# An expert's tokens by an indirect row transfer and transposes in place of a gather by products

## The reference

```python
def moe_swiglu(u, w_router, b_router, w_gate, w_up, w_down):
    tok = u.reshape(bn * s, d)
    logits = tok.astype(f32) @ w_router.astype(f32) + b_router.astype(f32)
    top_val, top_idx = lax.top_k(logits, TOP_K_EXPERTS)
    gates = jax.nn.softmax(top_val, axis=-1)
    combine = jnp.einsum('tk,tke->te', gates, jax.nn.one_hot(top_idx, N_EXPERTS, dtype=f32))
    out = jnp.zeros((bn * s, d), f32)
    for e in range(N_EXPERTS):
        out = out + combine[:, e:e + 1] * swiglu(tok, w_gate[e], w_up[e], w_down[e]).astype(f32)
    return out.astype(u.dtype).reshape(bn, s, d)
```

## Time and profile before

| what | value |
| --- | --- |
| median of 3 runs | 1637.91 us (1637.24 to 1638.79) |
| the profiled execution | 1632.35 us, span 1630.5 us |
| PE, PE weight loads | busy 94%, 73% of the span |
| DVE, ACT, POOL | busy 77%, 64%, 4% |
| DMA | 469.68 MB, mean 288 GB/s |
| PE's share of the chain that ended last | 81% |

### The profile page before, as it was taken

The page is one execution under the profiler, slowest core; times in us unless marked ns, Lnnn a source line. Parts: engine busy times, 40 slices in busy tenths (PEclk is TensorE's granted clock), DMA queues, the critical chain, the costliest instruction groups (busy, mean ns, idle before and its releaser), DMA issues.

```text
span 1630.5 us, 22147 instructions
## 1 busy us (share of the span) xinstructions
PE 1538.7 (94%) x7571; PEld 1195.2 (73%) x7572; DVE 1254.6 (77%) x1707; ACT 1048.2 (64%) x1381; POOL 62.8 (4%) x90
## 2 busy tenths in 40 slices
PE   4999989999799969999999999999999999999997
PEld 2645468887675458888888888888888888888885
DVE  6896345543682249899899889889989989989987
ACT  3105444443548437787788788788788778778775
POOL 5351000000000000000000000000000000000000
PEclk9999999999899969999999999999999999999998
DMA  9625876544458458999999999999989999999960
GB/s 321 239 104 199 317 283 212 178 179 166 150 178 309 156 219 308 348 353 359 337 356 351 367 340 343 367 334 348 379 321 352 364 332 367 348 337 362 357 255 27
DMA packets 203752, 469.68 MB, mean 288 GB/s; under 512 B 5108, under 2 KB 11558, under 8 KB 203574
## 3 DMA queue, kind: packets, MB, share of 16 engines
q1 hardware_dynamic: 202656, 466.80, 78.8%
q0 software_dynamic: 400, 1.09, 0.3%
q10 hardware_dynamic: 646, 1.16, 0.2%
HBM read 467.98 MB, written 1.05 MB: 288 GB/s over the span
## 4 chain that ended last, share of the span: by engine, by line
PE 81%; ACT 5%; DVE 4%; issue 2%; ACTq 0%; DVEq 0%
PE ps L810 23%; PE ps L812 22%; PE ps L811 22%; PE ps L816 2%; PE ps L1370 2%; DVE w_lo L1949 2%; PE ps L1329 2%; PE ps L1083 1%; ACT work L1845 1%; PE ps L835 1%; ACT uT L1601 1%; ACT w_hi L1588 1%; ACT uT L1610 1%; PE ps L1439 0%; PE ps L1440 0%
## 5 line engine op out<-in xcount | busy, mean ns | idle before, releaser
L1949 DVE TENSOR_TENSOR w_lo<-ring,w_hi 128x1024 fp32r<-128x1024 f32 (+2 forms) x572 | 668.0, 1200 | 118.1 <-ACT w_hi L1588 99.0
L1588 ACT ACTIVATE w_hi<-ring 128x1024 fp32r<-128x1024 f32 (+2 forms) x572 | 595.4, 1045 | 215.2 <-PE ps L812 211.8
L810 PE MATMUL ps<-w_hi,e_hi 128*128 128x512 f32 x896 | 356.6, 398 | 9.7 <-DVE w_lo L1949 9.7
L812 PE MATMUL ps<-w_hi,e_lo 128*128 128x512 f32 x896 | 350.5, 391 | 0.0
L811 PE MATMUL ps<-w_lo,e_hi 128*128 128x512 f32 x896 | 349.6, 390 | 0.0
L1949 DVE TENSOR_TENSOR w_lo<-ring_more,w_hi 128x1024 fp32r<-128x1024 f32 x192 | 228.9, 1222 | 40.5 <-ACT w_hi L1588 38.1
L1588 ACT ACTIVATE w_hi<-ring_more 128x1024 fp32r<-128x1024 f32 x192 | 201.6, 1067 | 70.7 <-PE ps L812 70.7
L810 PEld LDWEIGHTS ps<-w_hi,e_hi 128*128 128x128 f32 x896 | 168.9, 189 | 46.3 <-DVE w_lo L1949 13.2
L812 PEld LDWEIGHTS ps<-w_hi,e_lo 128*128 128x128 f32 x896 | 168.5, 188 | 36.7
L811 PEld LDWEIGHTS ps<-w_lo,e_hi 128*128 128x128 f32 x896 | 169.0, 189 | 33.5
L810 PE MATMUL ps<-w_hi,eT_hi 128*128 128x512 f32 x448 | 176.5, 394 | 5.7 <-DVE w_lo L1949 5.7
(11 more groups left out here) (283 smaller groups left out, 1600.4 us busy)
## 6 DMA issues: line engine op xcount, KB each, us to landing
ring<-in_moe_w_gate SPq DMA_DIRECT2D x48, 2048.0 KB, 10.0
ring<-in_moe_w_up SPq DMA_DIRECT2D x40, 2048.0 KB, 10.2
ring<-in_moe_w_down SPq DMA_DIRECT2D x32, 2048.0 KB, 10.4
ring<-in_w_ada SPq DMA_DIRECT2D x24, 2048.0 KB, 9.3
ring_more<-in_moe_w_down SPq DMA_DIRECT2D x24, 2048.0 KB, 7.9
ring_more<-in_moe_w_up SPq DMA_DIRECT2D x16, 2048.0 KB, 10.3
ring_more<-in_moe_w_gate SPq DMA_DIRECT2D x8, 2048.0 KB, 9.6
ring<-in_ff_w_gate SPq DMA_DIRECT2D x5, 2048.0 KB, 7.8
```

Of the source, the lines that this page charges most:

```text
L810: mm(o, xh, wh, start=start, stop=False)
L812: return mm(o, xl, wh, start=False, stop=stop)
L1588: fn(w, src, ACT.Copy).then_inc(hi_ready, 1)
L1949: V.tensor_tensor(w_lo[0:n, c, 0:f], src, w_hi[0:n, c, 0:f].bitcast(F32), ALU.subtract).then_inc(lo_ready, 1)
```

## The change

The normalised tokens `hn` are also stored in memory (`hn_rows`, 1 MB), once, by GpSimd. In the loop PE does the two narrow products alone at the end of b = 3 (`slot_tokens`). DVE copies the token numbers from bank 3 as integers into `slot_index` at b = 4. GpSimd then issues an indirect transfer that brings 128 rows of 4 KB, named by `slot_index`, from `hn_rows` into `x_e`, as rows. At the end of b = 4 PE waits for these rows and transposes the eight 128x128 blocks into banks 6 and 7, where the products wrote before. `slots_in` moves from b = 4 to b = 5 and writes over `x_e`. The gather ahead of the loop stays a product. The transfer of `g_final` stands behind the eight indirect transfers in GpSimd's stream.

```diff
+        slot_index = sb("slot_index", [P, 1], U32)
+        hn_rows = nc.dram_tensor("hn_rows", (S, D), F32, kind="Internal").ap()
...
+            pool.wait_ge(hn_ready, NT * 4)
+            pool.dma_start(hn_rows.rearrange("(t p) d -> p t d", p=P), hn).then_inc(rows_stored, 16)
+            pool.wait_ge(rows_stored, 16)
+            x_rows = x_e.rearrange("p k s -> p (k s)")
+            for e in range(E):
+                pool.wait_ge(slot_index_ready, e + 1)
+                pool.indirect_dma_start(x_rows, None, hn_rows[:, :], bass.IndirectOffsetOnAxis(ap=slot_index[:, 0:1], axis=0)).then_inc(rows_gathered, 16)
+
             pool.wait_ge(h_ready, 12)
             pool.dma_start(gate_row[:, 0, :], A["g_final"].unsqueeze(0).broadcast_to([P, D])).then_inc(late_in, 16)
...
                         for t in range(NT):
                             w = mm(o, hn[:, t, d], sel[:, t, :], start=t == 0, stop=t == NT - 1)
                     w.then_inc(gather_done, 1)
+                slot_tokens()
+
+            def slot_tokens():
+
                 for t in range(NT):
                     w = mm(ps[3][:, 0:2], sel[:, t, :], info[:, t, :], start=t == 0, stop=t == NT - 1)
                 w.then_inc(info_done, 1)
...
                     if b == 3 and gather_next:
+                        pe.wait_ge(sel_ready, g + 2)
+                        pe.wait_ge(selT_ready, job + 2)
+                        slot_tokens()
+                    if b == 4 and gather_next:
                         pe.wait_ge(scatter_added, job * 4 + 4)
-                        gather(g + 1)
+                        pe.wait_ge(rows_gathered, g * 16 + 16)
+                        for bank in range(2):
+                            for k in range(4):
+                                w = tr(ps[6 + bank][:, k * P:(k + 1) * P], x_e[:, 4 * bank + k, :])
+                            w.then_inc(gather_done, 1)
...
-                    if b == 4 and gather_next:
+                    if b == 5 and gather_next:
                         slots_in(g + 1)
...
                     convert("gate", b, (1, 2, 3))
+                    if b == 4 and gather_next:
+                        dve.wait_ge(info_done, g + 2)
+                        V.tensor_copy(slot_index[:, :], ps[3][:, 0:1]).then_inc(slot_index_ready, 1)
                     convert("up", b, (0, 1))
```

More of the change, by code:

```diff
@@ L331, in trunk @@
         gather_done = sem("gather_done")
+        rows_stored, slot_index_ready, rows_gathered = sem("rows_stored"), sem("slot_index_ready"), sem("rows_gathered")
         qi_copied, qi_ready, ki_ready = sem("qi_copied"), sem("qi_ready"), sem("ki_ready")
```

## The result

The changed kernel takes 1614.1 us (median of 4 runs, 1612.1 to 1618.6) against 1638.2 us, a ratio of 0.986 (95% interval 0.983 to 0.988). The prediction was 1615.7 us. The profiled execution took 1612.1 us with a span of 1610.3 us, 20.2 us less than the span before.

A forecast was written before the change was run, and what follows sets the result against it. PE was taken as the bound, the converters waiting for it. Per expert 4.03 us removed less 0.46 and 0.79 us added saves 2.78 us, times 8 is 22.2 us: 1637.9 - 22.2 = 1615.7 us, range 1611 to 1630.

The forecast's parts named there:

- 4.03: PE time per expert of the loop's gather and token products, with the longer step behind them, in us: removed.
- 0.46: PE time per expert of the two token products staying at the end of b = 3: 0.37 + 0.09 us.
- 0.79: PE time per expert of eight transposes at the end of b = 4: 0.70 + 0.09 us, upper end 0.97.
- The unpaid edits: Row transfer, index copy, slots_in move, hn store and g_final's later transfer were all costed at nothing.
- The budget of the rows: From index ready to PE's transposes at the end of b = 4: 14.7 us, against a landing of 6 to 11.
- The index copy: VectorE's copy in b = 4: 0.15 us, hidden in 11.4 us of idle; at worst 1.2 us in all.
- The stall behind `slots_in`: PE's 0.87 us stall behind ACT's eight writes, expected to move one block later at no more cost.
- Rival 1: Rows come late for the transposes, PE stalls 6.5 us per expert: 1667.7 us; chance 9%.
- Rival 4: GpSimd's descriptors wait 7.1 us for VectorE's conversions, rows come 2.7 us late: 1637.5 us, no change; chance 4%.
- Rival 2: Transfers are the bound in the loop at 351 GB/s, 1.3 us more per expert: 1648 us; chance 3%.
- Rival 3: Converters lose their rest around the gather, the slots_in burst costs 1.4 us more per expert: 1627 us; chance 12%.
- Rival 5: Transfer ceiling at the loop's best rate, 357 GB/s, only 0.8 us less per expert: 1631.3 us; chance 2%.

The follow-up runs named there:

- the half gather: The kernel before with only the first token half in the loop's product gather, 8 products instead of 16: 1623.2 us, ratio 0.991.
- the move: The kernel before with the product gather moved to the end of b = 4 and slots_in to b = 5, nothing else: 1636.9 us, ratio 0.9995.
- the added bytes: The changed kernel with four more indirect transfers of 512 KB per expert, behind the one that is needed: 1615.8 us, ratio 0.987.

## Why the prediction was right

**The bound.** PE paid for each record. Shown by the half gather (1.79 us counted, 1.76 us measured) and by the move, which changed nothing.

**The saving.** Forecast 4.03 - 0.46 - 0.79 = 2.78 us per expert; measured 125.63 - 122.97 = 2.66 us. The term that was mis-sized is the transposes: 0.79 us was taken, 0.88 us was paid, inside the bounds given (0.79 to 0.97). A transpose costs 0.11 us when the longer step behind the run is counted with it, so four are 0.35 + 0.09 = 0.44 us and eight 0.88 us. The sum doubled the 0.35 us and added the 0.09 us once. The other 0.03 us are below what the rows resolve. Times 8 the measured saving is 21.3 us, and the span fell by 20.2 us. The difference lies ahead of the loop: the last transposes of `hn` start at 580.93 instead of 580.12, before the store is even issued, at 581.17, and the token products ahead of the loop at 605.01 instead of 603.93. From there to the end it is 1005.3 us instead of 1026.6 us, 21.3 us less. The store costs nothing: from the token products ahead of the loop to the first ones in it the kernel before takes 74.8 us, and with the store added as well.

**The unpaid edits.** The budget of the rows was worked out as 14.7 us and is 14.7 us; the landing of 7.0 to 8.6 us is in the range taken, 6 to 11 us. The 14.7 us came out because its terms are distances of the old timeline with the gather taken out. None of the rows behind the range of the landing was of an indirect transfer, so that it held is in part luck. The index copy takes 0.15 us and is not seen in PE's waits. The stall behind `slots_in` moved by a block and kept its size, 1.10 us from product to product before and after.

**The rivals.** Rival 1 has the mechanism right: with the rows later than 14.7 us PE stands idle for the excess, eight times. Its price was too low, because it counted only the wait. With the lower clock behind it, rows that land 16.9 us after the index on average already cost what the change gains, where 17.5 us had been worked out as the point. Rival 4 has a mechanism that is there, the wait of an indirect issue for VectorE, but it had taken two runs of three conversions, 7.1 us, where the traces show the rest of one, at most 1.04 us. Rivals 2, 3 and 5 did not occur: the added bytes speak against 2 and 5, the half gather against 3.

**The median.** 1638.2 - 1614.1 = 24.1 us against 20.2 us in the profiled executions. Beside two of the experiments the same comparison gave 23.0 us. The loop gave 21.3 us of it. The four runs of the changed kernel spread over 6.5 us, which covers the rest, and the traces show where executions differ: over all the kernels the last transposes of `hn` start between 580.12 and 584.81 us, the earliest in the trace of the kernel before, while the expert periods of the kernel before agree within 0.01 us and those of the changed one within 0.1 us. So the spread lies ahead of the loop; what makes it was not looked into. That the median came out 1.6 us from the forecast although the saving was 0.9 us too high is luck within this spread.

## What to carry to other kernels

Where PE is the bound by the stretches and the waits, price an edit as PE records at the distance between their starts, with the longer step of the product behind them, and scale the two together. Work that replaces products may be slow on its own engine as long as its result has a measured budget: from the moment its input is ready to the moment PE gets there, in the timeline as it will be. Such a budget has a hard edge, so look at how much of it is left before adding to it.

## What the runs showed of the hardware

- An indirect transfer of 128 rows of 4 KB holds GpSimd for 0.94 us and lands after 7.0 to 8.6 us beside weight loads at 361 to 363 GB/s. It follows the load of the moment: over one such transfer the DMA share was 1.04 and it landed after 7.9 us; in the kernel before with the transfers added, where the issue comes later in the block, one landed after 5.3 us at a share of 0.74 (all eight: 4.6 to 5.8 us), and with the added bytes the one that is needed took up to 9.4 us.
- An indirect issue that begins while VectorE is in an instruction with both inputs in SBUF ends only 0.81 to 0.90 us after that instruction: 54 of 128 issues, up to 1.97 us long. A direct transfer does not wait (0.60 to 0.62 us, inside a conversion or not). The Trainium skill (SBUF — State Buffer, "Who interferes with whom") infers that tensor_tensor does not stop descriptors from being written; the direct transfers agree with that, the indirect ones did wait.
- VectorE is not slowed by the issues: with no transfer, one and five it is busy for 114.3 to 114.4 us of an expert, 93% of the time.
- After an idle of 8.5 to 10.3 us PE ran its transposes and three to ten products at the 1.2 GHz level. After idles of 2.0 to 3.1 us its transposes were slowed as well (1.3 to 1.6 us, granted clock 0.66 and 0.50), after those of 1.5 to 1.9 us they were not (0.85 us, granted clock 1.00).
- fp32 transposes of 128x128 at the 2.4 GHz level cost PE 0.11 us each, in runs of four, eight and sixteen.
- One core held 381 GB/s for two experts on end.
